# An expert's U row and V row fetched by one 8 KB gather into 16 pair buffers, with four blocks of diagonals

## Chip, cores and metric

One Trainium2 chip, of which the program uses one core. The metric is the time of the whole kernel on the device in microseconds (us); lower is better. All numbers are from timed runs or from one execution recorded by the hardware profiler.

## What is computed

A network of three layers on 256 tokens of width 1024, in float32. The part that the change touches is the expert layer at the end of the first block:

```python
# 256 tokens, 8 heads, 16 experts chosen per token and head out of 16384
ug = u_tab[ec]                     # rows of 1024 floats (4 KB)
vg = v_tab[ec]
act = gelu(einsum('thkd,td->thk', ug, xc))      # dot of each U row with its token
w = gc * act                                    # gate times activation
out = einsum('thk,thkd->td', w, vg)             # weighted sum of the V rows
```

The chosen experts come from scores against 2 x 128 sub-keys, top-16 of each half, top-16 of the 256 sums (the "routing"). What stands before it (two kinds of attention, projections) and behind it (a second block with attention, feed-forward layers) is not changed.

## The kernel before

The file is one straight program per engine, with semaphores between them. The expert stage is made of 16 **units**: unit u is one head of one half of the tokens (128 tokens, one in each partition; units 0 to 7 are tokens 0 to 127, units 8 to 15 the others). A unit has 16 experts per token, in 4 **blocks** of 4. One indirect DMA (a gather) brings, for one of the 16 experts, one row of 4 KB to each of the 128 partitions: 524,288 bytes. So a unit needs 16 gathers of U rows and 16 of V rows, 16.78 MB, and the stage 512 gathers.

Who does what for block b of unit u:

- **POOL** (GpSimd) issues the gathers, in one order: U block b of unit u, then V block b-1 (lines 644 to 667; V block 3 follows U block 0 of the next unit). U rows go to 8 buffers (`ubuf`, two blocks deep); before U block b POOL waits in `hold` until the dots of the block two before are done (`dots_done`). V rows go to 16 buffers (`vbuf`, four blocks deep); before V block b it waits until the same block of the unit before was summed (`rows_summed`, line 629). A unit's first U block also waits for its indices (`idx_ready`).
- **DVE** (VectorE) makes one dot for each gathered U row, in place in the row's buffer (line 1629, function `dot`; the tokens stand in PSUM), and between the dots, one piece behind each, the routing of the next unit and the one behind it (`route_stage`, lines 1544 to 1609; its pieces are chained by the semaphore `route_step`, raised and awaited by DVE itself). The indices of unit u+1 are done behind the fifth dot of unit u.
- **ACT** (ScalarE) turns the four dots into weights (gelu, line 928; times gate, line 933) and, in `diag` (line 942), the weights into four 128x128 diagonal matrices in `DIAG`. There are two blocks of diagonals, so `diag` of block b waits until block b-2 was summed (line 940). Once per unit it also makes the exponentials of the gates (line 924), on which DVE's `route_stage` 14 to 16 wait.
- **PE** (TensorE) adds, per gathered V row, diagonal times row into two PSUM banks (line 2333, `sum_rows`): 8 products of 128x128 by 128x512 in float32 for each block, each recorded as two instructions, and raises `rows_summed` behind the block. Before each row it waits for that row's landing (`v_loaded`).

The stage's surroundings. Unit 0 and 1 run while PE still makes queries and scores, units 2 to 15 stand in loops and, for the last two, behind them. Before unit 14 ACT and DVE do the normalization of the first half of the tokens (`norm_root`, `norm_rstd`), between units 14 and 15 they copy its transposed result (`norm_hi`, `norm_lo`). Behind unit 15 comes the input projection of the second block ("ab"): 14 pieces of weights, loaded by SP into the area that the expert rows leave, split into a high part by ACT (line 432) and a low part by DVE or POOL (line 439, 588). SP loads piece 0 when the dots of unit 15 block 2 are done, piece 1 with those of block 3 (lines 511 to 514), the others when the last V row has landed (line 515). ACT and DVE split piece 0 and 1 when block 0 and block 1 of unit 15 are summed (lines 981, 1695).

The place of things: `ROWS` is one area of 24,576 columns; `A`, `B` and the first half of `SCR` hold queries, sub-keys and scratch until the scores are made, and are free during the rest of the stage.

Of the kernel before, what the change touches and what calls it, by code (L numbers as in the profile page):

```python
# [15 lines left out]
D = 1024  # L16
# [8 lines left out]
UNITS = TT * PH  # L25
# [115 lines left out]
def build(nc, a, out, at):  # L141
    ctx = ExitStack()
    with ctx:
        sems = {}

        def sem(name):
            if name not in sems:
                sems[name] = ctx.enter_context(nc.semaphore(name))
            return sems[name]
# [119 lines left out]
        SCORE = PROJ[:, 0:4096]  # L269
        N2W = PROJ[:, 4096:5120]  # L270
        HEAD = PROJ[:, 5120:5632].rearrange("p (t n) -> p t n", t=TT)
        DIAG = PROJ[:, 5120:6144].rearrange("p (q k n) -> p q k n", q=2, k=4)
        R = PROJ[:, 6144:7168]
        r_s = R[:, 0:256].rearrange("p (q n) -> p q n", q=2)
        r_w = R[:, 256:512]
# [17 lines left out]
        ubuf = [ROWS[:, n * D:(n + 1) * D] for n in range(NU)]  # L293
        vcol = [NU + 8 * (n % 4 // 2) + 2 * (n // 4) + n % 2 for n in range(NV)]
        vbuf = [ROWS[:, c * D:(c + 1) * D] for c in vcol]
        XP_BANK = (J["peer_0"] + 6) % 8
        assert XP_BANK < 7
        XP = PS[:, XP_BANK:XP_BANK + 2, :]
# [37 lines left out]
        xn_ready = [sem(f"xn_ready{t}") for t in range(TT)]  # L336
        u_loaded = [sem(f"u_loaded{n}") for n in range(NU)]
        v_loaded = [sem(f"v_loaded{n}") for n in range(NV)]

# [114 lines left out]
        def _(sp):  # L454
# [53 lines left out]
            sp.wait_ge(*pieces["query", 1].used)  # L508
            for n in range(6, 8):
                load("query", n)  # L510
            sp.wait_ge(sem("dots_done"), 4 * UNITS - 1)
            load("ab", 0)
            sp.wait_ge(sem("dots_done"), 4 * UNITS)
            load("ab", 1)
            sp.wait_ge(v_loaded[NV - 1], 16 * UNITS)
            for p in range(2, 14):
                load("ab", p)
            sp.wait_ge(sem("h_logf"), 1)
# [61 lines left out]
        def _(pool):  # L580
# [45 lines left out]
            def values(u, q, b, first=False):  # L626

                if not first:
                    hold("rows_summed", u * 4 + (b - 3))
                elif b == 1:  # L630
                    for p in (6, 7):
                        w = pieces["query", p]
                        pool.wait_ge(hi_ready[w.h], w.count)
                        pool.wait_ge(lo_ready[w.h], w.count)
                else:
                    pool.wait_ge(*pieces["query", (0, 1, 6, 7)[b]].used)
                for k in range(4):
                    n = 4 * b + k
                    nc.gpsimd.indirect_dma_start(  # L639
                        out=vbuf[n], out_offset=None, in_=a["peer_v"][0],  # L640
                        in_offset=bass.IndirectOffsetOnAxis(ap=r_idx[:, q, n:n + 1], axis=0)
                    ).then_inc(v_loaded[n], 16)

            def unit(u, q, first=False, second=False):
# [21 lines left out]
                if first:  # L666
                    values(u, q, 3, first)

            unit(0, 0, first=True)
            unit(1, 1, second=True)  # L670
            with pool.Fori(1, UNITS // 2) as i:
                unit(i * 2, 0)
                unit(i * 2 + 1, 1)
            values(UNITS - 1, 1, 3)

            pool.wait_ge(sem("rows_summed"), 4 * UNITS)
            for p in (2, 3, 5, 7, 9, 11, 13):
# [42 lines left out]
        def _(act):  # L720
# [216 lines left out]
            def diag(u, b, wait=True):  # L937
                act.wait_ge(sem("weights_ready"), u * 4 + (b + 1))
                if wait:
                    act.wait_ge(sem("rows_summed"), u * 4 + (b - 1))  # L940
                for k in range(4):
                    ins = nc.scalar.activation(DIAG[:, b % 2, k, :], ident, ACT.Copy, scale=r_wt[:, b % 2, k:k + 1])  # L942
                ins.then_inc(sem("diag_ready"), 1)

            def act_unit(u, q, last=False):
# [21 lines left out]
            query_cols(7)  # L967
            for b in range(2, 4):
                weights(0, 0, b)
                diag(0, b)  # L970
            act_unit(1, 1)
            with act.Fori(1, UNITS // 2 - 1) as i:
                act_unit(i * 2, 0)
# [3 lines left out]
            norm_hi(2, 0)  # L977
            act_unit(UNITS - 1, 1, last=True)

            for p in halves(0):  # L980
                act.wait_ge(sem("rows_summed"), 4 * UNITS - 3 + p)
                split("ab", p)
            sqrt_table()
            act.wait_ge(sem("rows_summed"), 4 * UNITS - 1)
            split("ab", 2)
            norm_hi(2, 1)
            norm_root(2, 1, added(J["peer_1"]), added(J["peer_1"] + 1))
            act.wait_ge(sem("rows_summed"), 4 * UNITS)
            for p in range(3, 10):
                split("ab", p)  # L990

# [195 lines left out]
        def _(v):  # L1187
# [435 lines left out]

            def dot(u, b, k, tokens=XP):

                n = (4 * b + k) % NU
                rows = ubuf[n].rearrange("p (m n) -> p m n", m=2)
                v.wait_ge(u_loaded[n], u * 32 + 16 * (1 + b // 2))
# [62 lines left out]
            vec_unit(UNITS - 2, 0, start=False)  # L1691
            norm_lo(2, 0)
            vec_unit(UNITS - 1, 1, finish=False, start=False)
            for p in halves(0):
                v.wait_ge(sem("rows_summed"), 4 * UNITS - 3 + p)
                split_lo(v, "ab", p)
            for m in range(2):
                residual(J["peer_1"] + m, 1, m)
# [298 lines left out]
        def _(pe):  # L1997
# [323 lines left out]
            def sum_rows(u, t, last=False):  # L2321

                for b in range(4):
                    if last and b == 2:
                        for _ in range(4):
                            for acc in accs:
                                pe.matmul(acc[:, 0:S], zeros, C[:, 0:S], start=False, stop=False, skip_group_check=True)
                    pe.wait_ge(sem("diag_ready"), u * 4 + (b + 1))
                    for k in range(4):
                        n = 4 * b + k  # L2330
                        pe.wait_ge(v_loaded[n], u * 16 + 16)
                        for m in range(2):
                            ins = pe.matmul(PS[:, (J[f"peer_{t}"] + m) % 8, :], DIAG[:, b % 2, k, :],  # L2333
                                            vbuf[n][:, m * BANK:(m + 1) * BANK], start=False, stop=False, skip_group_check=True)
                    ins.then_inc(sem("rows_summed"), 1)

            for t in range(TT):
                accs = [bank(J[f"peer_{t}"] + m) for m in range(2)]
                for acc in accs:
                    pe.matmul(acc, zeros, C[:, 0:BANK], start=True, stop=False, skip_group_check=True)  # L2340
                with pe.Fori(t * PH // 2, (t + 1) * PH // 2 - t) as i:
# [314 lines left out]
```

## Time and profile before

| | |
|---|---|
| timed runs | 1562.36, 1563.62, 1566.21 us; median 1563.62 |
| the profiled execution | span from first to last instruction 1649.9 us; its device time is not given beside the span |
| span over the median | 86.3 us |
| TensorE clock, mean granted | 0.928 of full |
| busy in the span | PE 1384.1, DVE 1022.0, POOL 820.8, ACT 704.8 us |
| DMA | 414.99 MB, of which gathers 268.47 MB |
| expert stage | first gather issued at 178 us, last block summed at 943 us |

The profile is read from the page (totals, the span in 40 slices, the queues) to the stage (a table of busy time over chosen stretches, one for each unit), and from there to the single instructions in order of time with what ended the idle time before each. A releaser called "remote" is one that the trace has no record for.

### The profile page before, as it was taken

The page shows a single profiled execution, that of the slowest core. Times are in us where ns is not written, and L with a number is a line of the kernel's source. Part 1 is how long each engine was busy: PE and PEld are TensorE (multiplying, and loading weights), DVE is VectorE, ACT ScalarE, POOL GpSimd, SP SyncE. Part 2 cuts the span into 40 slices and gives each one's busy share as a digit, 9 for nine tenths or more (in the row PEclk, how much of TensorE's full clock was granted, in tenths as well). Part 3 has the DMA queues.
Part 4 walks back from the last instruction along what each step waited for, and adds up shares of the span by engine and source line. Part 5 has one row for each costly group of instructions (what it writes and reads, how often), then busy time and mean ns, then how long its engine had stood idle before and what let it go on. Part 6 is the DMA issues. An engine that isn't in the chain of part 4 may idle for free.

```text
span 1649.9 us, 18659 instructions
## 1 busy us (share of the span) xinstructions
PE 1384.1 (84%) x5985; PEld 974.4 (59%) x5985; DVE 1022.0 (62%) x1923; ACT 704.8 (43%) x1374; POOL 820.8 (50%) x789
## 2 busy tenths in 40 slices
PE   7999986566775876765566899999999998999998
PEld 6777942222332332332232487979888877888887
DVE  4986875665565655655544454766885478488833
ACT  5445521321222221222232337247764657576634
POOL 2332767566766666666646462105552533164514
PEclk9999998778887888887788999999999999999999
DMA  8294899999999999999979961156766552277650
GB/s 316 71 193 145 278 355 375 342 364 392 364 357 366 356 364 372 357 349 351 349 270 374 358 222 32 51 154 188 209 190 210 179 205 77 77 209 199 208 206 26
DMA packets 217026, 414.99 MB, mean 252 GB/s; under 512 B 13210, under 2 KB 117250, under 8 KB 216962
## 3 DMA queue, kind: packets, MB, share of 16 engines
q0 software_dynamic: 73728, 268.47, 42.7%
q1 hardware_dynamic: 143090, 145.66, 28.7%
q8 instruction: 37, 0.61, 0.2%
q14 instruction: 27, 0.22, 0.0%
q10 hardware_dynamic: 144, 0.04, 0.0%
HBM read 409.93 MB, written 4.19 MB: 251 GB/s over the span
## 4 chain that ended last, share of the span: by engine, by line
PE 35%; another core or an unknown queue 20%; DVE 9%; ACT 9%; issue 8%; POOL 4%; DMA 1%; POOLq 0%; ACTq 0%; DVEq 0%
PE ps L2500 9%; PE ps L2333 5%; PE ps L2049 5%; PE ps L2501 5%; PE ps L2051 5%; PE ps L2050 5%; DVE expert_rows L1629 3%; ACT proj L942 2%; POOL weights_lo L588 2%; ACT weights_hi L432 2%; ACT proj L933 1%; DVE weights_lo L439 1%; POOL ple_proj_lo L588 1%; DMA expert_rows<-in_peer_v,route_idx 1%
## 5 line engine op out<-in xcount | busy, mean ns | idle before, releaser
L2333 PE MATMUL ps<-expert_rows,proj 128*128 128x512 f32 x1024 | 487.8, 638 | 223.8 <-ACT proj L942 182.0
L2333 PEld LDWEIGHTS ps<-expert_rows,proj 128*128 128x128 f32 x1024 | 208.0, 206 | 502.9 <-issue 320.2
L1629 DVE CUSTOM_DVE_ANT_0 expert_rows<-expert_rows,ps 128x1024 f32<-128x1024 f32 x240 | 290.2, 1212 | 116.3 <-DMA expert_rows<-in_peer_u,route_idx 87.1
L588 POOL TENSOR_TENSOR weights_lo<-weights_raw,weights_hi 128x512 fp32r<-128x512 f32 x120 | 160.2, 1369 | 364.3 <-ACT weights_hi L432 322.3
L658 POOL DMA_INDIRECT expert_rows<-in_peer_u,route_idx x256 | 249.9, 976 | 130.8 <-issue 77.7
L639 POOL DMA_INDIRECT expert_rows<-in_peer_v,route_idx x256 | 247.7, 967 | 132.0 <-issue 73.4
L942 ACT ACTIVATE proj<-consts,proj 128x128 f32<-128x128 f32 x256 | 81.8, 390 | 458.7 <-remote 338.1
L432 ACT CAST weights_hi<-weights_raw 128x2048 fp32r<-128x2048 f32 x98 | 185.5, 1916 | 103.5 <-PE ps L2051 79.1
L2500 PE MATMUL ps<-x_normT,weights_hi 128*128 128x512 f32 x640 | 222.5, 392 | 0.0
L439 DVE TENSOR_TENSOR weights_lo<-weights_raw,weights_hi 128x2048 fp32r<-128x2048 f32 x68 | 161.5, 2381 | 73.2 <-ACT weights_hi L432 72.8
L2049 PE MATMUL ps<-weights_hi,x_normT 128*128 128x512 f32 (+1 forms) x496 | 188.4, 380 | 10.2 <-DVE weights_lo L439 3.9
L2051 PE MATMUL ps<-weights_hi,x_normT 128*128 128x512 f32 (+1 forms) x496 | 184.8, 373 | 0.0
L2050 PE MATMUL ps<-weights_lo,x_normT 128*128 128x512 f32 (+1 forms) x496 | 184.6, 372 | 0.0
L2501 PE MATMUL ps<-x_normT,weights_lo 128*128 128x256 f32 x640 | 179.2, 280 | 0.0
L2500 PEld LDWEIGHTS ps<-x_normT,weights_hi 128*128 128x128 f32 x640 | 119.7, 187 | 26.3
L2501 PEld LDWEIGHTS ps<-x_normT,weights_lo 128*128 128x128 f32 x640 | 121.0, 189 | 0.0
L2049 PEld LDWEIGHTS ps<-weights_hi,x_normT 128*128 128x128 f32 x496 | 93.4, 188 | 32.3 <-issue 4.4
L2051 PEld LDWEIGHTS ps<-weights_hi,x_normT 128*128 128x128 f32 x496 | 93.4, 188 | 16.7
L2050 PEld LDWEIGHTS ps<-weights_lo,x_normT 128*128 128x128 f32 x496 | 93.5, 189 | 15.5 <-issue 0.2
L1861 DVE SCALAR_TENSOR_TENSOR work_a<-ps,conv_cols,work_a 128x254 f32<-128x254 f32 (+1 forms) x176 | 76.5, 476 | 29.2 <-ACT work_a L1077 25.1
L695 POOL TENSOR_TENSOR hidden_hi<-work_a 128x256 f32 (+1 forms) x44 | 41.9, 951 | 100.2 <-ACT work_a L1057 100.0
L2049 PE MATMUL ps<-weights_hi,hidden_hi 128*128 128x512 f32 x176 | 68.7, 390 | 0.0
(340 smaller groups left out, 1959.3 us busy)
## 6 DMA issues: line engine op xcount, KB each, us to landing
weights_raw<-in_ffn_up SPq DMA_DIRECT2D x88, 512.0 KB, 5.0
weights_raw<-in_ffn_down SPq DMA_DIRECT2D x22, 1024.0 KB, 4.9
weights_raw<-in_ab_w_in SPq DMA_DIRECT2D x14, 1024.0 KB, 5.2
weights_raw<-in_w_in SPq DMA_DIRECT2D x12, 1024.0 KB, 9.2
weights_raw<-in_ple_gate SPq DMA_DIRECT2D x8, 1024.0 KB, 6.2
weights_raw<-in_c_w_in SPq DMA_DIRECT2D x6, 1024.0 KB, 6.2
weights_raw<-in_w_out SPq DMA_DIRECT2D x4, 1024.0 KB, 17.7
weights_raw<-in_peer_w_query SPq DMA_DIRECT2D x4, 1024.0 KB, 8.2
```

What stands on the lines that cost most here:

```text
L432: copy(w.hi[:, :], w.raw[:, :]).then_inc(hi_ready[w.h], 1)
L439: eng.tensor_tensor(w.lo[:, :], w.raw[:, :], w.hi[:, :].bitcast(F32), ALU.subtract).then_inc(lo_ready[w.h], 1)
L588: ins = pool.tensor_tensor(w.lo[:, c], w.raw[:, c], w.hi[:, c].bitcast(F32), ALU.subtract)
L639: nc.gpsimd.indirect_dma_start(out=vbuf[n], out_offset=None, in_=a["peer_v"][0], in_offset=bass.IndirectOffsetOnAxis(ap=r_idx[:, q, n:n + ...
L658: nc.gpsimd.indirect_dma_start(out=ubuf[n], out_offset=None, in_=a["peer_u"][0], in_offset=bass.IndirectOffsetOnAxis(ap=r_idx[:, q, 4 * b ...
L1629: ins = nc.vector.tensor_tensor_reduce(out=rows, in0=rows, in1=tokens, scale=1.0, scalar=0.0, op0=ALU.mult, op1=ALU.add, accum_out=r_dot[: ...
L2049: pe.matmul(o, x[0], w[0], start=first, stop=False)
L2050: pe.matmul(o, x[0], w[1], start=False, stop=False)
L2051: return pe.matmul(o, x[1], w[0], start=False, stop=last)
L2333: ins = pe.matmul(PS[:, (J[f"peer_{t}"] + m) % 8, :], DIAG[:, b % 2, k, :], vbuf[n][:, m * BANK:(m + 1) * BANK], start=False, stop=False, ...
L2500: pe.matmul(b.rearrange("p (a t) -> p a t", a=2), hi[:, c, g, :], x_both(c), start=c == 0, stop=False)
L2501: ins = pe.matmul(b[:, 0:S], lo[:, c, g, :], XHI[:, c, :], start=False, stop=c == KC - 1)
```

## The change

A new input, `peer_uv`, holds for each expert its U row and its V row side by side (8 KB). Units 0 and 1 work as before. From unit 2 to unit 14 one gather brings the pair for one expert, so a unit has 16 gathers, of 1,048,576 bytes each. There are 16 pair buffers of 8 KB per partition, four blocks deep: four of them in `A`, `B` and `SCR`, twelve in `ROWS`. Before block b POOL waits until the same block of the unit before was summed. Unit 15 (`last_unit`) again gathers U and V rows apart, each into its half of a pair buffer, in the order of before. `DIAG` has four blocks, so ACT's `diag` waits for the block four before. PE waits for V landings in units 0, 1 and 15 alone. The first loads of "ab" wait until block 1 of unit 15 is summed, and their splits until block 2 is, since these areas now hold pairs.

```diff
-        DIAG = PROJ[:, 5120:6144].rearrange("p (q k n) -> p q k n", q=2, k=4)
+        DIAG = [x[:, n * BANK:(n + 1) * BANK].rearrange("p (k n) -> p k n", k=4)
+                for x in (PROJ[:, 5120:6144], SCR[:, 2048:3072]) for n in range(2)]
...
+        pair_buf = [A[:, 0:HALF], A[:, HALF:2 * HALF], B[:, 0:HALF], SCR[:, 0:HALF]]
+        pair_buf += [ROWS[:, n * HALF:(n + 1) * HALF] for n in (0, 1, 2, 3, 4, 8, 5, 9, 6, 10, 7, 11)]
...
-            sp.wait_ge(sem("dots_done"), 4 * UNITS - 1)
-            load("ab", 0)
-            sp.wait_ge(sem("dots_done"), 4 * UNITS)
-            load("ab", 1)
-            sp.wait_ge(v_loaded[NV - 1], 16 * UNITS)
+            sp.wait_ge(sem("rows_summed"), 4 * UNITS - 2)
+            for p in halves(0):
+                load("ab", p)
+            sp.wait_ge(v_loaded[NV - 1], 48)
...
+            def pairs(u, q, first=False):
+
+                hold("idx_ready", u + 1)
+                for b in range(4):
+                    if first and b == 0:
+                        pool.wait_ge(pe_done, END["score_rest"])
+                    elif first and b == 1:
+                        pool.wait_ge(sem("dots_done"), 4 * u)
+                    else:
+                        hold("rows_summed", 4 * u if first and b == 3 else u * 4 + (b - 3) + (1 if first else 0))
+                    for k in range(4):
+                        n = 4 * b + k
+                        gather(pair_buf[n], a["peer_uv"], q, n, pair_loaded[n])
+
+            def last_unit(u, q):
+
+                pool.wait_ge(sem("idx_ready"), u + 1)
+                for b in range(5):
+                    if b < 4:
+                        pool.wait_ge(sem("rows_summed"), u * 4 + b - 3)
+                        for n in range(4 * b, 4 * b + 4):
+                            gather(pair_buf[n][:, 0:D], a["peer_u"][0], q, n, pair_loaded[n])
+                    if b > 0:
+                        for n in range(4 * b - 4, 4 * b):
+                            gather(pair_buf[n][:, D:2 * D], a["peer_v"][0], q, n, v_loaded[n])
+
             unit(0, 0, first=True)
             unit(1, 1, second=True)
-            with pool.Fori(1, UNITS // 2) as i:
-                unit(i * 2, 0)
-                unit(i * 2 + 1, 1)
-            values(UNITS - 1, 1, 3)
+            values(1, 1, 3)
+            pairs(2, 0, first=True)
+            pairs(3, 1)
+            with pool.Fori(2, UNITS // 2 - 1) as i:
+                pairs(i * 2, 0)
+                pairs(i * 2 + 1, 1)
+            pairs(UNITS - 2, 0)
+            last_unit(UNITS - 1, 1)
...
             def diag(u, b, wait=True):
                 act.wait_ge(sem("weights_ready"), u * 4 + (b + 1))
                 if wait:
-                    act.wait_ge(sem("rows_summed"), u * 4 + (b - 1))
+                    act.wait_ge(sem("rows_summed"), u * 4 + (b - 3))
...
+            act.wait_ge(sem("rows_summed"), 4 * UNITS - 1)
             for p in halves(0):
-                act.wait_ge(sem("rows_summed"), 4 * UNITS - 3 + p)
                 split("ab", p)
             sqrt_table()
-            act.wait_ge(sem("rows_summed"), 4 * UNITS - 1)
+            act.wait_ge(sem("rows_summed"), 4 * UNITS)
             split("ab", 2)
...
+                    rows = pair_buf[n][:, 0:D]
+                    v.wait_ge(pair_loaded[n], u * 16 - 16)
...
                     for k in range(4):
                         n = 4 * b + k
-                        pe.wait_ge(v_loaded[n], u * 16 + 16)
+                        if early or last:
+                            pe.wait_ge(v_loaded[n], 48 if last else u * 16 + 16)
+                        rows = vbuf[n] if early else pair_buf[n][:, D:2 * D]
...
+    given += [("peer_uv", _np.concatenate([inputs["peer_u"][0], inputs["peer_v"][0]], 1))]
```

## Rows read from the trace of the kernel before

**Rows 1.** The page: DMA busy in 40 slices of the span, in tenths.
```profile
DMA  8294899999999999999979961156766552277650
```

**Rows 2.** Busy time by stretch, one row each for units 0 and 5.
```profile
core 0: us, PE busy (x) PEld busy (x) DVE busy (x) ACT busy (x) POOL busy (x), PEclk, DMA share, GB/s
178.00:229.00 51.00, 43.80 (x313) 38.87 (x312) 43.67 (x87) 20.41 (x37) 41.49 (x32) 0.97 0.94 339
...
414.00:460.00 46.00, 30.50 (x65) 13.18 (x65) 26.29 (x72) 11.84 (x40) 30.83 (x33) 0.80 0.94 365
```

**Rows 3.** POOL in order of time: last gather of a run, and the next.
```profile
452.67 0.94 POOL L658 DMA_INDIRECT expert_rows<-in_peer_u,route_idx  x1 [0.30 <-issue]
459.33 0.94 POOL L639 DMA_INDIRECT expert_rows<-in_peer_v,route_idx  x1 [5.72 <-remote]
```

**Rows 4.** Busy time by stretch: DMA at full rate, and behind the hold.
```profile
437.00:457.00 20.00, 7.47 (x18) 3.04 (x16) 9.90 (x31) 0.00 (x0) 12.65 (x14) 0.75 1.03 409
457.00:462.00 5.00, 2.05 (x3) 1.02 (x4) 4.17 (x13) 3.31 (x13) 2.06 (x3) 0.50 0.44 149
```

**Rows 5.** DVE and ACT in order of time, around the hold.
```profile
443.59 0.41 DVE L1569 TENSOR_TENSOR proj<-proj 128x256 f32<-128x256 f32 x1
...
451.45 0.43 DVE L1572 MAX8 proj<-proj 128x8 f32<-128x256 f32 x1 [4.54 <-remote]
...
458.62 1.28 ACT L942 ACTIVATE proj<-consts,proj 128x128 f32<-128x128 f32 x4 [21.72 <-remote]
```

**Rows 6.** PE in order of time, and two short stretches of it.
```profile
414.01 30.45 PE L2333 MATMUL ps<-expert_rows,proj 128*128 128x512 f32 x64 [16.39 <-ACT proj L942]
...
414.00:421.00 7.00, 6.99 (x10) 3.06 (x11) 7.00 (x19) 3.13 (x14) 5.48 (x6) 0.61 0.78 263
430.00:437.00 7.00, 7.00 (x17) 3.04 (x16) 2.45 (x8) 2.22 (x9) 5.23 (x6) 1.00 1.03 414
```

**Rows 7.** POOL's waits in the stage: us in total, times, longest.
```profile
POOL expert_rows L639 <- remote: 57.7, 12, 5.7
POOL expert_rows L658 <- DVE proj L1629: 37.4, 8, 15.7
POOL expert_rows L658 <- remote: 11.3, 3, 6.2
```

**Rows 8.** The page: packet sizes; two queues (packets, MB, share of 16 engines).
```profile
DMA packets 217026, 414.99 MB, mean 252 GB/s; under 512 B 13210, under 2 KB 117250, under 8 KB 216962
...
q0 software_dynamic: 73728, 268.47, 42.7%
q1 hardware_dynamic: 143090, 145.66, 28.7%
```

**Rows 9.** One block of unit 14 on ACT and PE, in order of time.
```profile
858.02 0.20 ACT L928 ACTIVATE proj<-proj 128x4 f32<-128x4 f32 x1 [3.44 <-DVE proj L1629]
858.32 0.85 ACT L933 ACTIVATE proj<-proj 128x1 f32<-128x1 f32 x4
859.20 1.28 ACT L942 ACTIVATE proj<-consts,proj 128x128 f32<-128x128 f32 x4
...
860.53 7.13 PE L2333 MATMUL ps<-expert_rows,proj 128*128 128x512 f32 x16 [1.68 <-ACT proj L942]
```

**Rows 10.** POOL's two long holds near the end, and what DVE waited for.
```profile
858.79 0.94 POOL L658 DMA_INDIRECT expert_rows<-in_peer_u,route_idx  x1 [15.67 <-DVE proj L1629]
904.60 0.94 POOL L658 DMA_INDIRECT expert_rows<-in_peer_u,route_idx  x1 [6.29 <-DVE proj L1629]
...
851.78 0.17 DVE L1269 RECIPROCAL stats<-stats 128x1 f32<-128x1 f32 x1 [23.82 <-ACT stats L772]
```

**Rows 11.** The end of the stage: PE, ACT, DVE in order of time.
```profile
943.58 0.47 PE L2049 MATMUL ps<-weights_hi,x_normT 128*128 128x512 f32 x1
...
940.78 1.90 ACT L432 CAST weights_hi<-weights_raw 128x2048 fp32r<-128x2048 f32 x1 [5.70 <-issue]
...
942.80 2.29 DVE L439 TENSOR_TENSOR weights_lo<-weights_raw,weights_hi 128x2048 fp32r<-128x2048 f32 x1 [5.30 <-ACT weights_hi L432]
```

More of the change, by code:

```diff
@@ L338, in build @@
         v_loaded = [sem(f"v_loaded{n}") for n in range(NV)]
+        pair_loaded = [sem(f"pair_loaded{n}") for n in range(NV)]
         def cols512(m, c0, n=512):
@@ L667, in unit, with gather @@
                     values(u, q, 3, first)
+            def gather(dst, table, q, n, loaded):
+                nc.gpsimd.indirect_dma_start(
+                    out=dst, out_offset=None, in_=table, in_offset=bass.IndirectOffsetOnAxis(ap=r_idx[:, q, n:n + 1], axis=0)
+                ).then_inc(loaded, 16)
+            def pairs(u, q, first=False):
[20 more added lines that the diff above has]
+                            gather(pair_buf[n][:, D:2 * D], a["peer_v"][0], q, n, v_loaded[n])
             unit(0, 0, first=True)
             unit(1, 1, second=True)
-            with pool.Fori(1, UNITS // 2) as i:
-                unit(i * 2, 0)
-                unit(i * 2 + 1, 1)
-            values(UNITS - 1, 1, 3)
+            values(1, 1, 3)
[6 more added lines that the diff above has]
+            last_unit(UNITS - 1, 1)
             pool.wait_ge(sem("rows_summed"), 4 * UNITS)
@@ L939, in diag @@
                 if wait:
-                    act.wait_ge(sem("rows_summed"), u * 4 + (b - 1))
+                    act.wait_ge(sem("rows_summed"), u * 4 + (b - 3))
                 for k in range(4):
-                    ins = nc.scalar.activation(DIAG[:, b % 2, k, :], ident, ACT.Copy, scale=r_wt[:, b % 2, k:k + 1])
+                    ins = nc.scalar.activation(DIAG[b][:, k, :], ident, ACT.Copy, scale=r_wt[:, b % 2, k:k + 1])
                 ins.then_inc(sem("diag_ready"), 1)
@@ L969, in _ @@
                 weights(0, 0, b)
-                diag(0, b)
+                diag(0, b, wait=False)
             act_unit(1, 1)
@@ L987, in _ @@
             norm_root(2, 1, added(J["peer_1"]), added(J["peer_1"] + 1))
-            act.wait_ge(sem("rows_summed"), 4 * UNITS)
             for p in range(3, 10):
@@ L1624, in dot @@
             def dot(u, b, k, tokens=XP):
-                n = (4 * b + k) % NU
-                rows = ubuf[n].rearrange("p (m n) -> p m n", m=2)
-                v.wait_ge(u_loaded[n], u * 32 + 16 * (1 + b // 2))
+                n = 4 * b + k
+                if isinstance(u, int) and u < 2:
+                    rows = ubuf[n % NU]
+                    v.wait_ge(u_loaded[n % NU], u * 32 + 16 * (1 + b // 2))
+                else:
+                    rows = pair_buf[n][:, 0:D]
+                    v.wait_ge(pair_loaded[n], u * 16 - 16)
+                rows = rows.rearrange("p (m n) -> p m n", m=2)
                 ins = nc.vector.tensor_tensor_reduce(out=rows, in0=rows, in1=tokens, scale=1.0, scalar=0.0,
@@ L1693, in _ @@
             vec_unit(UNITS - 1, 1, finish=False, start=False)
+            v.wait_ge(sem("rows_summed"), 4 * UNITS - 1)
             for p in halves(0):
-                v.wait_ge(sem("rows_summed"), 4 * UNITS - 3 + p)
                 split_lo(v, "ab", p)
@@ L2328, in sum_rows @@
                     pe.wait_ge(sem("diag_ready"), u * 4 + (b + 1))
+                    early = isinstance(u, int) and u < 2
                     for k in range(4):
                         n = 4 * b + k
-                        pe.wait_ge(v_loaded[n], u * 16 + 16)
+                        if early or last:
+                            pe.wait_ge(v_loaded[n], 48 if last else u * 16 + 16)
+                        rows = vbuf[n] if early else pair_buf[n][:, D:2 * D]
                         for m in range(2):
-                            ins = pe.matmul(PS[:, (J[f"peer_{t}"] + m) % 8, :], DIAG[:, b % 2, k, :],
-                                            vbuf[n][:, m * BANK:(m + 1) * BANK], start=False, stop=False, skip_group_check=True)
+                            ins = pe.matmul(PS[:, (J[f"peer_{t}"] + m) % 8, :], DIAG[b][:, k, :],
+                                            rows[:, m * BANK:(m + 1) * BANK], start=False, stop=False, skip_group_check=True)
                     ins.then_inc(sem("rows_summed"), 1)
@@ L2340, in _ @@
                     pe.matmul(acc, zeros, C[:, 0:BANK], start=True, stop=False, skip_group_check=True)
-                with pe.Fori(t * PH // 2, (t + 1) * PH // 2 - t) as i:
+                for u in range(0 if t else 2):
+                    sum_rows(u, t)
+                with pe.Fori(PH // 2 if t else 1, (t + 1) * PH // 2 - t) as i:
                     sum_rows(i * 2, t)
```

## Prediction, made before the changed kernel was run

> **What bounds the kernel now.** I read the page first: DMA is busy nine tenths and more through the slices of the expert stage and idle or half idle elsewhere, where PE is full [rows 1]. So the stage (763 us of the span, first gather to last landing) is where the change can count, and it is made of transfers. Next the table by unit: a middle unit takes 46 us, in which DVE works 26, PE 30, ACT 12, POOL 31 us, and the DMA engines 94% at 365 GB/s [rows 2]. No computing engine is full. Then single instructions. POOL issues a gather every 1.245 us (0.94 plus 0.30 of idle) [rows 3]: 32 of them are 39.8 us. The DMA engines at their fullest, share 1.03, move 409 GB/s [rows 4]: 16.78 MB are 41.0 us. These two are nearly equal, and a unit is 46 because POOL then holds 5.72 us [rows 3]. It holds once in most units, 69 us in 15 holds, beside 37.4 us in 8 holds for DVE's dots [rows 7], and the DMA engines run dry behind it (share 0.44, 149 GB/s) [rows 4].
>
> What the hold waits for is strange. DVE's MAX8 at 451.45 needs only the semaphore that DVE's own instruction of 443.59, ended at 444.00, raised; it starts 7.4 us later. ACT's diagonals at 458.62 waited 21.7 us for a sum that PE's records end by 444.5 [rows 5, 6]. Both come through "remote", in the stretch where DMA is at full rate, and POOL is released just when the engines run dry. So in this execution semaphores arrive late while DMA is full. I take this for an effect of recording, because the span is 86.3 us above the median of the timed runs, and the holds called remote are 69 us, with more behind them at unit 14. A timed run then spends 763 - 86.3 = 676.7 us in the stage. It can be checked: unit 0 as recorded, 51 us (POOL's issues are longer there) [rows 2], and 15 units at 41.0 are 666; 10.7 us are left for holds that are real. **A timed unit is thus bound by the DMA engines at about 41.0 us, with POOL at 39.8 just under it**, and not by the holds that fill the profile. I therefore make the sum against the 1563.6 of the timed runs; against the profiled 1649.9 the same terms would give 86 us more at each place, if recording costs as much again. This is the step I trust least, and the first rival takes its opposite.
>
> **POOL.** Units 2 to 14, 13 units, have 16 gathers in place of 32: POOL's issue falls from 39.8 to 19.9 us per unit if a pair costs as much as a row (as many indices and rows; the size alone differs), at most 39.8 again if an 8 KB row is written as two. On a timed run's path this is nothing at either end, since DMA needs 41.0; but POOL can now run ahead, and what it waits for is no longer the dots.
>
> **DMA.** The bytes of a unit stay. The packets fall from 32 x 128 rows and 32 x 16 semaphore writes to half of both, 2304 fewer, 144 per engine. What does one cost beyond its bytes? The queue of the gathers holds 73,728 packets of 3,641 bytes in the mean and took 42.7% of 16 x 1649.9 us: 152.9 ns each. The other has 143,090 of 1,018 bytes in 28.7%: 52.9 ns each [rows 8]. The line through both is 38.1 ns per 1,000 bytes and 14 ns per packet. That is the upper bound, as small packets also wait. The lower one comes from the full rate: at 409 GB/s an engine takes 160 ns for 4,096 bytes, of which 156 are bytes by that slope, so 4 ns. I take the middle, 9 ns: 144 x 9 = 1.3 us per unit (0.6 to 2.0), 13 x 1.3 = **-17 us** (-8 to -26). Unit 41.0 becomes 39.7.
>
> Two statements of the Trainium skill, DMA: Bandwidth & Descriptors, bear on this. Its section on where 436 GB/s comes from says that for HBM to SBUF the HBM side binds at about 358 GB/s; by that a unit would be 46.9 us before and after, and packets would be worth nothing; the 409 GB/s of [rows 4] speak against it for this core alone. The same section has the ports end at 435 GB/s; by that a unit could not fall under 38.6 us, and 13 units would give at most 31 us.
>
> **Depth.** Before, U runs two blocks ahead, and the queue is shallow, since POOL is only 3% faster than DMA. DVE's pauses reach POOL and then DMA: 15.67 us before unit 14, where DVE stood 23.8 us for ACT's root, and 6.29 at unit 15 [rows 10]. After, a block's four buffers are refilled when it is summed, with three blocks, 3 x 9.9 = 29.7 us of transfers, still to come. From landing to sum it takes: last dot 1.2 and a routing piece 0.7, gelu, weights, diagonals 0.20 + 0.85 + 1.28, PE 7.1 [rows 9], 11.4 us, and POOL's 1.2 to the first refill. If PE stands at its lower clock, a block costs 7.0 / 10 x 16 = 11.2 us at a granted 0.61 and by that up to 13.7 at 0.5 [rows 6]: 19 us. At full clock 29.7 - 12.6 = 17 us are left, more than either hold as recorded; at the lower clock 10, more than the shorter. So the real part of these holds goes. Of the 10.7 us left over above, 7 us may be a hold in unit 0 to 1, which stays; I take **-5 us** for the rest (0 to -11).
>
> PE itself: 4 x 6.9 = 27.5 us per unit at full clock against 39.7 us, 70%. It was 30.5 in 46 with the clock falling each time it stood for 16 us [rows 2, 6]; with a block every 9.9 us its pauses are 3 us. It would bound only at the low clock held throughout (55 us), which its own work prevents: over a stretch that starts 16 us later it is 1.00 again [rows 6]. DVE has 26 and ACT 12 us of work per unit [rows 2]. The four blocks of diagonals cost no instruction; ACT's wait for PE moves two blocks back.
>
> **The seam at unit 2.** V block 3 of unit 1 now goes ahead of unit 2, whose first pair block waits for the scores (long made), the second for unit 1's dots, the third and fourth for its last sum. The U rows of those dots are issued 12 gathers (15 us) before POOL asks; the last sum comes 2.3 + 7.1 = 9.4 us behind the last dot [rows 9], while the first two pair blocks hold 19.8 us of transfers. I take 0 for a gap, at most 3 us. Queued behind that wait are only POOL's own gathers.
>
> **The end.** Unit 15 has the order and bytes of before. Piece 0 of "ab" is loaded later and piece 1 earlier (both at the sum of block 1), and both are split behind the sum of block 2: 1.9 + 1.9 + 2.3 = 6.1 us against 7.1 us of PE for block 3 [rows 9, 11]. Before, piece 1 was cast at 940.78 and its low part came at 942.80, while PE began at 943.58 [rows 11]. The cover is block 3; if the loads come late, piece 1 gates PE. Within -1 to +4 us; I take 0.
>
> Sum: 1563.6 - 17 - 5 = **1542 us**, ends 1563.6 - 26 - 11 = 1527 and 1563.6 - 8 + 7 = 1563.
>
> **The rivals.** *Late semaphores are real, and now never drained.* For: [rows 3 to 6]; DMA will be full without a pause, and recovery came only when it ran dry. If a timed run has them, a block's way from landing to refill is 13 + 21 = 34 us, over the 29.7 us that are covered; it decides from about 17 us of lateness on. A unit would take 9.9 + 34 + 3 = 47 us against 41: +78 us for 13 units, 1640 us. Against: the 676.7 us leave no room for them before. 8%.
>
> *A row still moves as before.* If a gather's 8 KB row is cut into two 4 KB packets, or bytes alone set the rate, the packets save nothing but semaphore writes, and only the depth is left: 1563.6 - 0 to -5, 1560 us. For: nearly all packets are under 8 KB [rows 8], so no gather shows the price. Against: 217,026 - 216,962 = 64 are 8 KB or more, so such packets exist. The Trainium skill (same page, section SWDGE vs HWDGE vs iDMA) prefers packets of at most 4096 B. By that POOL would need 39.8 us again too. 12%.
>
> *8 KB packets or the seam and end cost more than they give*, a few us slower: 1563.6 + 10, 4%. *The timed run had holds of its own*: then up to 676.7 - (51 + 41 + 13 x 39.0 + 41) = 37 us go, 1527. This is in my range and has 10%.
>
> **How the numbers follow.** The forecast has 66%. A measurement of this kernel can tell about 0.3%, 4.7 us. Faster: 66 + 10 and 3 of the second rival, 79%; same: its other 9%; slower: 8 + 4, 12%. The range 1526 to 1565 holds the forecast's bounds, the deep gain and the second rival, and leaves out the first.
>
> **What the changed profile would show.** POOL's gathers at 1.24 us, 16 per unit, and long waits for PE's sums (over 15 us per unit), not for dots. DMA share 1.0 with about 420 GB/s in any 20 us of units 3 to 14; no dip near unit 14; the first load of "ab" behind a PE sum. Recorded semaphores may still come late there, and its span may stand above its timed runs by 80 us or more. I am wrong if POOL's gather takes 1.9 us, if the rate stays at 409, if the timed gain is near 80 us (then the holds were real), or if units end in waits at a full DMA.

## The result, and the profile after

The changed kernel takes **1548.39 us** in the median (4 runs, 1547.70 to 1549.62), beside 1562.99 us (4 runs, 1561.88 to 1566.21) for the kernel before on the same chip: ratio 0.9895, interval 0.9873 to 0.9918. The forecast was 1542, its range 1526 to 1565. The profiled execution has a span of 1547.8 us and its own time is 1549.62 us, so this time nothing lies between profiled and timed runs.

The page of the changed kernel: DMA busy in 40 slices, the sizes of packets and the queue of the gathers (packets, MB, share of 16 engines), and the group of the pair gathers (count, busy us, mean ns, idle before it).

```profile
DMA  9286699999999999999999500557665443476650
...
DMA packets 187077, 415.00 MB, mean 268 GB/s; under 512 B 9883, under 2 KB 113923, under 8 KB 160387
...
q0 software_dynamic: 43776, 268.45, 42.3%
...
L674 POOL DMA_INDIRECT expert_rows<-in_peer_uv,route_idx x156 | 148.3, 951 | 229.7 <-PE ps L2379 193.4
```

Against [rows 1] the weak slice near unit 14 is gone. The slices are of different lengths (41.2 us before, 38.7 after), so they are compared by shape alone. Against [rows 8] the queue of the gathers lost 29,952 packets, which is 13 units x 2304: an 8 KB row moves as one packet. A pair gather holds POOL for 951 ns, no more than a row of 4 KB in [rows 3].

Busy time by stretch, changed kernel: the seam, a stretch of the middle, and the last stretch, where unit 15 gathers its rows apart again.

```profile
270.00:345.00 75.00, 59.46 (x124) 24.37 (x122) 47.26 (x122) 19.61 (x65) 31.05 (x34) 0.93 1.01 421
...
385.00:425.00 40.00, 29.93 (x64) 12.39 (x64) 27.38 (x70) 12.35 (x41) 15.15 (x16) 0.96 1.01 421
...
785.00:825.00 40.00, 33.74 (x77) 15.61 (x78) 25.02 (x48) 13.11 (x52) 24.34 (x26) 0.91 1.02 410
```

Each stretch of 40 us from 345 to 785 shows 420 to 422 GB/s, where [rows 4] has 409 at its fullest. Cut at every 16.78 MB of landed rows, units 2 to 14 take 39.8 to 40.0 us each. POOL's waits in the stage (us in total, times, longest) and some of its gathers in order of time:

```profile
POOL expert_rows L674 <- PE ps L2379: 196.2, 40, 8.2
POOL work_a L674 <- PE ps L2379: 69.8, 13, 9.1
```

```profile
344.07 1.10 POOL L674 DMA_INDIRECT expert_rows<-in_peer_uv,route_idx  x1 [3.54 <-PE ps L2379]
345.47 0.94 POOL L674 DMA_INDIRECT expert_rows<-in_peer_uv,route_idx  x1 [0.30 <-issue]
346.71 0.93 POOL L674 DMA_INDIRECT expert_rows<-in_peer_uv,route_idx  x1 [0.30 <-issue]
347.95 0.94 POOL L674 DMA_INDIRECT expert_rows<-in_peer_uv,route_idx  x1 [0.30 <-issue]
355.70 0.94 POOL L674 DMA_INDIRECT expert_rows<-in_peer_uv,route_idx  x1 [6.81 <-PE ps L2379]
```

POOL now waits 266 us for sums, about 20 us per unit, and it costs nothing: DMA has share 1.01 all the while. No wait is called remote in this trace from 270 to 830 us, against 69 us of such holds in [rows 7] alone.

### The profile page after: what moved, and what is told of

The parts are those of the page before. It is cut to its first block, busy times and chain, and to the rows that moved or that the text cites. A ratio compares the mean times of both kernels' runs of the same rounds, so it can differ in the third digit from the quotient of the medians.

```text
span 1547.8 us, 18260 instructions
## 1 busy us (share of the span) xinstructions
PE 1387.3 (90%) x5985; PEld 971.1 (63%) x5985; DVE 1032.8 (67%) x1923; ACT 707.7 (46%) x1374; POOL 622.3 (40%) x581
## 4 chain that ended last, share of the span: by engine, by line
PE 51%; DMA 21%; DVE 9%; POOL 7%; ACT 6%; issue 5%; ACTq 0%; POOLq 0%; DVEq 0%
DMA expert_rows<-in_peer_uv,route_idx 15%; PE ps L2548 10%; PE ps L2379 9%; PE ps L2092 7%; PE ps L2094 7%; PE ps L2093 7%; DMA scratch<-in_peer_uv,route_idx 5%; PE ps L2549 5%; DVE weights_lo L443 2%; POOL weights_lo L591 2%; POOL expert_rows L642 2%; ACT weights_hi L436 1%; POOL expert_rows L674 1%; PE ps L2057 1%; POOL expert_rows L661 1%
## 5 line engine op out<-in xcount | busy, mean ns | idle before, releaser
L1672 DVE CUSTOM_DVE_ANT_0 expert_rows<-expert_rows,ps 128x1024 f32<-128x1024 f32 x184 | 224.1, 1220 | 142.6 <-DMA expert_rows<-in_peer_uv,route_idx 131.6
L2379 PE MATMUL ps<-expert_rows,scratch 128*128 128x512 f32 x512 | 241.9, 629 | 58.3 <-ACT scratch L981 58.3
L674 POOL DMA_INDIRECT expert_rows<-in_peer_uv,route_idx x156 | 148.3, 951 | 229.7 <-PE ps L2379 193.4
L2379 PEld LDWEIGHTS ps<-expert_rows,scratch 128*128 128x128 f32 x512 | 100.6, 201 | 198.6 <-issue 118.9
L967 ACT ACTIVATE proj<-proj 128x4 f32<-128x4 f32 x64 | 13.2, 206 | 402.1 <-DVE proj L1672 402.1
L2379 PE MATMUL ps<-expert_rows,proj 128*128 128x512 f32 x288 | 136.9, 632 | 27.4 <-ACT proj L981 27.4
L2379 PEld LDWEIGHTS ps<-expert_rows,proj 128*128 128x128 f32 x288 | 57.1, 202 | 107.4 <-issue 69.2
L2379 PE MATMUL ps<-work_a,proj 128*128 128x512 f32 x112 | 62.8, 713 | 33.6 <-ACT proj L981 33.6
```

The source lines that it names most:

```text
L674: nc.gpsimd.indirect_dma_start(out=dst, out_offset=None, in_=table, in_offset=bass.IndirectOffsetOnAxis(ap=r_idx[:, q, n:n + 1], axis=0)). ...
L2379: ins = pe.matmul(PS[:, (J[f"peer_{t}"] + m) % 8, :], DIAG[b][:, k, :], rows[:, m * BANK:(m + 1) * BANK], start=False, stop=False, skip_gr ...
```

## The experiments

The runs were made on three chips, each beside runs of the kernel before on the same chip. On the first the kernel before takes 1565.33 us (17 runs, 1561.31 to 1568.46), on the second 1663.36 us (11 runs, 1651.89 to 1675.33), on the third 1655.31 us (15 runs, 1643.20 to 1663.86). That difference turned out to be the main finding. On which chip the first result was measured is not on record. Its times for the kernel before, 1561.88 to 1566.21 us, are those of the first chip, and the text counts it with that one.

### The kernel before once more, on the first chip

> The kernel before, unchanged, profiled a second time. Theory A (the late semaphores and POOL's hold of 5.7 us per unit belong to that one recording, a timed run does not have them): the timed run is again 1562 to 1566 us, and if this recording is clean its span is within 3 us of that, its middle units take 40.9 to 41.2 us, POOL's waits called remote are gone, and the last gather lands near 852 us. Theory B (the holds are part of the kernel): the span is again near 1650 us with units of 46 us, while the timed run stays at 1563, and then only recording can explain the 86 us.

Measured: 2285.11 us (1 run). In it the chip granted TensorE a mean clock of 0.556, so it says nothing of the 1563 us. No wait of its stage is called remote, but DMA is at 0.93 there and not full. It gives one price:

```profile
500.00:549.00 49.00, 49.00 (x65) 14.48 (x64) 25.77 (x69) 11.60 (x39) 30.34 (x32) 0.56 0.93 338
```

At 0.56, close to the lower of the two clock levels, PE is busy for all of the 49 us and a unit takes 49.1 us. The prediction had 55 us for a PE held at its low clock, but that was for a granted 0.5: its 27.5 us of work at full clock, divided by 0.56, are 49 us.

### Two 4 KB gathers in place of one of 8 KB, first chip

```diff
-                        gather(pair_buf[n], a["peer_uv"], q, n, pair_loaded[n])
+                        gather(pair_buf[n][:, 0:D], a["peer_u"][0], q, n, pair_loaded[n])
+                        gather(pair_buf[n][:, D:2 * D], a["peer_v"][0], q, n, pair_loaded[n])
```

> The changed kernel, but each pair fetched by two gathers of 4 KB rows, U and V, into the two halves of the same pair buffer; buffers, waits and four blocks of diagonals as in the change. Theory packets (the gain is the longer row: 39.8 instead of 41.0 us per unit): 13 units x 1.2 = 16 us come back, 1562 to 1566 us, units of 40.9 to 41.1 us. Rival depth (the gain is POOL running ahead and the deeper buffers): it keeps most of the gain, 1548 to 1553 us.

Measured: 1563.52 us (8 runs), ratio 0.9981 (0.9970 to 0.9992) to the kernel before. One stretch, and POOL's waits for PE in the stage:

```profile
340.00:380.00 40.00, 30.97 (x63) 12.62 (x62) 26.07 (x61) 12.11 (x39) 30.16 (x33) 0.91 1.03 410
```

```profile
POOL expert_rows L674 <- PE ps L2380: 8.5, 12, 3.6
POOL work_a L674 <- PE ps L2380: 6.5, 4, 3.9
```

All that the change has but the 8 KB gather is here, and the rate is 410 GB/s and a unit 41.0 us, as before. So the 1.2 us per unit come from the 8 KB rows, not from buffers or waits. Cut by landed rows, this kernel takes 801.9 - 269.0 = 532.9 us from the start of unit 2 to that of unit 15, and the changed one 787.9 - 270.2 = 517.7 us: 15.2 us in 13 units, 1.17 us each.

### Four blocks of diagonals alone, first chip

```diff
-        DIAG = PROJ[:, 5120:6144].rearrange("p (q k n) -> p q k n", q=2, k=4)
+        DIAG = [x[:, n * BANK:(n + 1) * BANK].rearrange("p (k n) -> p k n", k=4)
+                for x in (PROJ[:, 5120:6144], SCR[:, 2048:3072]) for n in range(2)]
...
-                    act.wait_ge(sem("rows_summed"), u * 4 + (b - 1))
+                    act.wait_ge(sem("rows_summed"), u * 4 + (b - 3))
```

> The kernel before with the four blocks of diagonals alone. Theory packets: no change, 1562 to 1565 us. Rival depth (ACT's early wait for PE held the stage back): 3 to 8 us faster, 1555 to 1560 us.

Measured: 1567.81 us (10 runs), ratio 1.0014 (1.0002 to 1.0027): worth nothing. This is also the first readable profile of the old order of gathers on this chip: a stretch, and POOL's waits in the stage other than its own issue.

```profile
500.00:541.00 41.00, 32.58 (x71) 13.91 (x70) 26.13 (x68) 12.01 (x39) 30.71 (x32) 0.89 1.03 409
```

```profile
POOL expert_rows L659 <- DVE proj L1630: 9.1, 8, 1.6
POOL expert_rows L640 <- DVE proj L1630: 4.0, 13, 0.3
```

Its own time is 1564.13 us. It was profiled too, and yet every unit from 1 to 14 takes 40.9 to 41.1 us, no wait is called remote, no hold for dots is longer than 1.6 us, and nothing dips before unit 14. So recording alone does not make the holds of [rows 3]. That the four diagonals took them away is the rival, and the same kernel on the third chip, below, speaks against it.

### Two blocks of diagonals in the changed kernel, first chip

```diff
-                    act.wait_ge(sem("rows_summed"), u * 4 + (b - 3))
+                    act.wait_ge(sem("rows_summed"), u * 4 + (b - 1))
...
-                    ins = nc.scalar.activation(DIAG[b][:, k, :], ident, ACT.Copy, scale=r_wt[:, b % 2, k:k + 1])
+                    ins = nc.scalar.activation(DIAG[b % 2][:, k, :], ident, ACT.Copy, scale=r_wt[:, b % 2, k:k + 1])
```

> The changed kernel with two blocks of diagonals instead of four. Theory packets: PE works 30 of 40 us in blocks of 7.1 us that come every 9.9 us, so ACT never waits for the block two before; no change, 1547 to 1550 us. Rival depth: 3 us and more are lost, over 1551 us.

Measured: 1546.98 us (4 runs), ratio 0.9877 (0.9860 to 0.9893): no worse than the change itself. ACT waits for DVE's dots in both (349.7 and 352.3 us from 300 to 820), so the diagonals of two blocks before are long free.

This run shows where the changed kernel's profiled execution loses 3 us behind the stage. PE in order of time, first the changed kernel, then this one, in the same short products of the second block:

```profile
971.11 0.49 PE L2215 MATMUL ps<-proj,expert_rows 128*128 128x128 f32 x2
971.53 0.43 PE L2219 MATMUL ps<-expert_rows,work_b 128*64 128x128 f32 x2
971.89 0.80 PE L2215 MATMUL ps<-proj,expert_rows 128*128 128x128 f32 x2
...
978.65 1.97 PE L2057 MATMUL ps<-consts,x_norm 128*128 128x128 f32 x8
```

```profile
971.34 0.49 PE L2215 MATMUL ps<-proj,expert_rows 128*128 128x128 f32 x2
...
975.27 1.09 PE L2057 MATMUL ps<-consts,x_norm 128*128 128x128 f32 x8
```

A pair of products goes from 0.49 to 0.80 us in the middle of a row of equal ones: from 971 to 980 the changed kernel was granted 0.55, this one 1.00. The first run with two gathers has the same fall at 986 us, without the 8 KB rows. Whether the other runs of the change had it is not known: they take 1547.70 to 1548.89 us, those with two blocks of diagonals 1546.80 to 1548.82.

### The kernel before on the second chip

> The kernel before, unchanged, once more, since the recording before it fell on a chip that granted 0.556 of the clock throughout. Theory A (POOL's hold of 5.7 us per unit belonged to the first recording alone): span within 3 us of the timed 1562 to 1568, middle units of 41.0 us, no wait of POOL called remote, last landing near 852 us, as the kernel with four blocks of diagonals alone already showed. Theory B: units of 46 us again.

Measured: 1667.66 us (1 run), and the 11 runs beside it, which left no profile, take 1651.89 to 1675.33 us. So here the long time is the kernel's, recorded or not. Its units 3 to 13 take 45.4 to 48.9 us. POOL's waits in the stage:

```profile
POOL expert_rows L639 <- remote: 54.1, 14, 5.5
POOL expert_rows L658 <- DVE proj L1629: 51.8, 14, 15.7
POOL expert_rows L658 <- remote: 18.2, 6, 5.3
```

They are like those of [rows 7]. Waits called remote are real on this chip and absent on the first; that a late semaphore stands behind one is shown closely further down.

### The changed kernel on the second chip

> The changed kernel, unchanged, for comparison on the same chip. 1547 to 1550 us, units of 39.8 us. If TensorE's low clock after unit 14 and in the second block was chance, it need not be in this recording, and the span is then up to 5 us shorter.

Measured: 1557.38 us (6 runs, 1551.41 to 1561.72), ratio 0.9369 (0.9329 to 0.9409): **a gain of 6.3% where the first chip gave 1.0%.** POOL's waits in its stage:

```profile
POOL expert_rows L674 <- PE ps L2379: 193.1, 37, 12.1
POOL work_a L674 <- PE ps L2379: 70.6, 12, 8.4
```

Waits called remote end in this trace around the seam, from 269 to 284 us (ACT once 17.51 us, POOL once 2.35 us); the last 4 KB row of unit 1 starts to move at 274. From 284 to 790 us, where only pairs move, there is one more, of 0.2 us at DVE. Units 1 and 2 take 45.4 and 41.9 us against 40.9 and 40.0 on the first chip, the others 39.8 to 39.9 us as there. The clock did not fall in the short products either: from 970 to 985 us PE was granted 1.00.

Unit 15 gathers 4 KB rows again, at the full rate:

```profile
815.00:825.00 10.00, 10.00 (x24) 4.37 (x23) 4.62 (x9) 2.33 (x9) 6.30 (x7) 1.00 1.03 409
```

No wait in it is called remote, and it takes 46.2 us here and 47.1 on the first chip. Two other traces of the changed kernel's variants on the slower chips have short holds of POOL there (2.4 to 3.2 us). So 4 KB rows at the full rate do not by themselves cost time on this chip. What else is needed is not shown.

### Without the zero products of unit 15, second chip

```diff
-                    if last and b == 2:
-                        for _ in range(4):
-                            for acc in accs:
-                                pe.matmul(acc[:, 0:S], zeros, C[:, 0:S], start=False, stop=False, skip_group_check=True)
```

These products add nothing; they stand in the kernel before too. In the changed kernel's trace on the first chip they lie on PE's path, since PE is behind the landings there:

```profile
815.40 7.03 PE L2379 MATMUL ps<-expert_rows,proj 128*128 128x512 f32 x16
822.27 3.62 PE L2370 MATMUL ps<-consts 128*128 128x256 f32 x16
825.72 13.90 PE L2379 MATMUL ps<-expert_rows,scratch 128*128 128x512 f32 x32
```

> The changed kernel without the eight products with zeros (3.6 us) that PE makes between block 1 and block 2 of unit 15. Theory (in the changed kernel the V rows of block 2 have landed by then, so these products lie on PE's path to the last sum): the last sum comes 2 to 3 us sooner behind the last landing, 1545.5 to 1547.5 us. Rival (the last landing sets the end in any case, as with two blocks of diagonals, or the clock falls for want of them): no change or up to 3 us slower.

Measured: 1556.97 us (6 runs), ratio 0.9369 (0.9329 to 0.9409), the same as the change. Without them PE stands idle for 3.14 us before its sums at 828.13, where the products had been, so on this chip they fill a wait. Whether they cost anything in the profile of the first chip, where PE was granted 0.68 just before, no run shows.

### Less depth, second chip

```diff
-                        hold("rows_summed", 4 * u if first and b == 3 else u * 4 + (b - 3) + (1 if first else 0))
+                        hold("rows_summed", u * 4 + (b - 1))
```

> The changed kernel, but in units 2 to 14 POOL waits before each block for the sum of the block two before, so that two blocks instead of four are in flight. Theory (a block's way from landing to refill is 11.4 + 1.2 us, which the other blocks' transfers have to cover): one block of 9.95 us covers too little, DMA runs dry, a block takes (9.95 + 12.6 + 1) / 2 = 11.8 us, a unit 47 us, the kernel 1548 + 13 x 7.3 = 1643 us, DMA share near 0.85. Rival (the refill is quicker than the records say, or PE's clock is low and makes it slower): under 1600 us, or over 1700 us.

Measured: 1744.62 us (1 run), 54.4 to 56.6 us in each of units 3 to 13. One turn of two blocks:

```profile
560.44 0.94 POOL L674 DMA_INDIRECT expert_rows<-in_peer_uv,route_idx  x1 [3.51 <-PE ps L2379]
...
577.40 0.21 ACT L967 ACTIVATE proj<-proj 128x4 f32<-128x4 f32 x1 [7.37 <-DVE proj L1672]
578.60 1.28 ACT L981 ACTIVATE proj<-consts,proj 128x128 f32<-128x128 f32 x4
...
579.93 7.13 PE L2379 MATMUL ps<-expert_rows,proj 128*128 128x512 f32 x16 [1.11 <-ACT proj L981]
...
587.99 0.94 POOL L674 DMA_INDIRECT expert_rows<-in_peer_uv,route_idx  x1 [3.71 <-PE ps L2379]
```

From a block's first gather to the gather that waits for its sum it takes 27.55 us, of which 10.6 us lie behind its last dot. The other 17.0 us are its issue, its transfer and the rest of the block before it, since POOL issues two blocks close together. Two blocks per 27.5 us are 55 us per unit, not the 47 expected from 12.6 us per way. The time is the one that the rival gave (over 1700 us), but its reason, a low clock, is not in these rows, since sums of 7.13 us are PE's at full clock. The same kernel with b - 2 in place of b - 1, on the third chip:

> The change, but POOL waits before block b for the sum of the block three before in place of the block four before, so only two blocks of transfers (2 x 9.95 = 19.9 us) cover the way from a block's last landing to its refill. By my 12.6 us for that way there is no hold that empties the queues and the time is that of the change, 1547 to 1560 us. With two blocks (the run before this) a block took 13.7 us in place of 9.95, so the way was about 27 us with one block still to come, or what was late there was something else. By 27 us, two covered blocks leave 7 us per block open and a unit takes (19.9 + 27 + about 0) / 3 x ... about 9.95 x 4 x 27 / 19.9 = 54 us at the worst, 1650 us or more; in between, 1560 to 1600 us, the way is 14 to 20 us.

Measured: 1550.07 us (1 run), units of 39.8 to 40.0 us from unit 3 on. One block more of depth takes back all of it. So by this run three blocks would do, and the fourth of the change is reserve.

### What keeps the change fast on the slower chips

Three kernels again, on the third chip, beside 1655.31 us for the kernel before. Two gathers in place of one:

> The change with its U and V row fetched by two gathers of 4 KB, a second time. On a chip where the kernel before takes 1561 to 1568 us it should again take about 1564. The run is for a chip where the kernel before takes 1650 us or more: there the changed kernel took 1557, and three things of it could protect it. If it is the new buffers and waits (POOL waits only for PE's sums, three blocks deep), this kernel has them too and takes 1565 to 1580 us. If it is the halved number of gathers, packets and semaphore writes, this kernel does not have that, POOL has again 39.8 us of gathers in a 41.0 us unit, and it takes 1630 to 1670 us. My guess is 60 to 40 for the buffers and waits.

Measured: 1640.08 us (7 runs), ratio 0.9921 (0.9878 to 0.9964). The guess, 60 to 40 for buffers and waits, was wrong. Four diagonals in the kernel before:

> The kernel before with four blocks of diagonals, a second time. On a chip where the kernel before takes 1561 to 1568 us: no change. Where it takes 1650 us or more: if the late diagonals alone (ACT waiting for PE) make POOL's holds, it falls to below 1600 us; if the holds come from dots and sums told late to POOL, as I think, it stays within 1 % of the kernel before.

Measured: 1640.78 us (9 runs), ratio 0.9925 (0.9889 to 0.9961), within the 1% expected. Two diagonals in the changed kernel:

> The change with two blocks of diagonals, a second time. On either kind of chip within 0.5 % of the change itself, 1545 to 1565 us, if the four blocks are worth nothing; above 1580 us on a chip where the kernel before takes 1650 us, if the two further blocks are what makes the change robust.

Measured: 1556.77 us (4 runs), ratio 0.9410 (0.9352 to 0.9468), as the change. The kernel with two gathers has the four diagonals too, so its 0.8% are no more than theirs: the new buffers and the new order add nothing here that can be told from noise. The rest of the 6% comes with the 8 KB gather, which the last of the three kernels has and the first two have not. The second also answers the rival left open on the first chip: with four diagonals, holds called remote are there all the same (POOL 50.8 us in 10 holds). The trace of the run with two gathers on this chip shows a hold closely: POOL, PE, DVE and ACT, each in order of time, and then two stretches by busy time.

```profile
549.46 0.94 POOL L674 DMA_INDIRECT expert_rows<-in_peer_v,route_idx  x1 [0.31 <-issue]
555.97 0.94 POOL L674 DMA_INDIRECT work_a<-in_peer_u,route_idx  x1 [5.57 <-remote]
...
529.21 5.15 PE L2380 MATMUL ps<-work_a,proj 128*128 128x512 f32 x8 [5.18 <-ACT proj L982]
534.20 1.88 PE L2380 MATMUL ps<-work_b,proj 128*128 128x512 f32 x4
535.91 1.88 PE L2380 MATMUL ps<-scratch,proj 128*128 128x512 f32 x4
...
546.99 0.08 DVE L1673 DVE_READ_ACCUMULATOR2_ANT proj<- 128x1 f32 x1
...
553.69 0.21 ACT L968 ACTIVATE proj<-proj 128x4 f32<-128x4 f32 x1 [14.35 <-remote]
```

```profile
530.00:550.00 20.00, 14.93 (x32) 6.03 (x30) 10.97 (x29) 2.33 (x9) 15.12 (x17) 0.93 1.03 410
550.00:556.00 6.00, 0.00 (x0) 0.00 (x0) 3.09 (x9) 2.17 (x9) 0.43 (x2) 0.50 0.86 342
```

The block in `work_a`, `work_b` and `scratch` was summed by 537.8. POOL was ready to refill it at 550.4 and went on at 555.97, 18.2 us behind the sum. Its other condition, the indices of the next unit, was met at 529.3. ACT's gelu came 6.6 us behind its last dot. DMA is at 1.03 up to 550, and both go on only when it is at 0.86. The changed kernel with two diagonals, on the same chip and at the same place of a unit:

```profile
576.16 1.88 PE L2379 MATMUL ps<-scratch,proj 128*128 128x512 f32 x4
...
578.87 0.94 POOL L674 DMA_INDIRECT work_a<-in_peer_uv,route_idx  x1 [3.72 <-PE ps L2379]
```

There the refill comes 0.8 us behind the sum, with DMA at 1.01 and 422 GB/s. What stays open is which part of the 8 KB gather does it. It halves the row packets, the semaphore writes of the queues and POOL's issuing at once; no run here separates them. Nor does a run show what makes a semaphore late, or in what the chips differ.

## Why the prediction was right, and where it was wrong

**The time and the bound: right.** A unit is bound by the DMA engines at 41.0 us with POOL just under it; the run with four diagonals shows 41.0 us and DMA at 1.03. That the timed comparison fell on a chip of the first kind is luck. On the second chip the changed kernel's 1557 us are still in the range, but the gain of 21 us that was forecast is 106 us there.

**The cause given for the 86.3 us: wrong.** The step that failed is "I take this for an effect of recording, because the span is 86.3 us above the median of the timed runs". Two chips on which this kernel takes 1643 to 1675 us in every run stand in its place, on one of them with the same holds in its trace. That the kernel of [rows 2 to 7] was recorded on such a chip is the plain reading, though its own time was not given. The difference between a profile and the timed runs was evidence that two conditions existed, not that one of them was the profiler's. The rival "late semaphores are real" had the right cause; it had the wrong outcome (1640 us), since in the stretch of 8 KB rows hardly a wait is late though DMA is full. The sign "I am wrong if the timed gain is near 80 us" did come, as 106 us, on the second chip.

**Packets: right, 15.2 us for 17.** 1.17 us per unit over 144 packets per engine is 8.1 ns each; the middle of 4 and 14 ns had been 9. One packet of 8 KB takes 313 ns in the median and one of 4 KB, in the run with two gathers, 161 ns, and the rate goes from 410 to 421 GB/s. The rival "a row still moves as before" falls with the packet count. The Trainium skill, DMA: Bandwidth & Descriptors, section SWDGE vs HWDGE vs iDMA, prefers packets of at most 4096 B; here 8 KB ones are the faster by 2.9% and need half of POOL's issues. The 358 GB/s that the Trainium skill gives for HBM to SBUF (same page, section Where 436 GB/s comes from) did not bind, as 421 GB/s show; its 435 for the ports was not reached.

**Depth: smaller than taken, and not where it was taken.** 2.9 us for 5: the last row lands at 852.0 us with the old order and at 849.1 with two gathers into the new buffers, one trace each. In timed runs these buffers are worth 1.8 us against the kernel before (1565.33 to 1563.52). Of the 2.9 us, 2.4 lie in unit 15 (49.6 us from its start to the last landing against 47.2), and none at the holds of [rows 10], which this chip doesn't have. The 5 us had no firm ground: 10.7 us less the 7 that may stay would have been 3.7.

**The seam: right.** POOL holds 6.84 us at 281.89, and DMA stays at 1.01 from 270 to 345.

**The end: 0 taken, 0 found in the stage.** From the last landing to the last sum it takes 4.6 us before (four diagonals) and 4.5 after. PE was granted 0.68 from 805 to 815 us, and its sums then run behind the landings. Behind it the low clock at 971 to 980 takes about 3 us. The sum on one profile each, from four diagonals in the kernel before to the change: last landing 852.0 to 835.0, -17.0; clock +3; -14. The times of these two executions are 1564.13 and 1549.62 us, -14.5. Of the 6 us between the forecast and the result, 2 are packets and 2 depth. The low clock would make up the rest, but it is read from one execution, and that the median run had it is not shown.

**PE and the way to a refill.** PE at a granted 0.56 takes 49.1 us per unit, which is the prediction's sum at that clock; its 55 us were for 0.5, which no run held. The way of 12.6 us from landing to refill was right for the part behind the dots, but counted from the gather it is 27.5 us when POOL issues in pairs of blocks; the three blocks of cover hide it with 29.7, and even two did.

## What to carry to other kernels

When rows that are used together lie apart in memory, put them side by side and gather them by one transfer: per byte it costs fewer packets, and it halves the issuing of a POOL that stood at 97% of the DMA time. When a profile and the timed runs differ by some per cent, time the kernel on another chip before the difference is put down to recording. And judge a change of a kernel with full DMA queues on more than one chip, as the same edit gave 1.0% on one and 6.3% on another.

## What the runs showed of the hardware that was not expected

- One program, three chips: 1561 to 1568 us on one and 1643 to 1675 us on the two others. On these, semaphores between engines arrive late while the DMA engines move 4 KB gathers at share 1.03: on the third chip POOL went on 18.2 us behind the sum that it waited for. In the stretch of 8 KB gathers, at 1.01, it was 0.8 us. One unit of 4 KB gathers at 1.03, unit 15 of the changed kernel, showed no such wait on the second chip.
- A gather of 128 rows holds POOL for 0.94 us and 0.30 of idle whether the rows have 4 or 8 KB.
- One run had TensorE at 0.556 of its clock from beginning to end and took 2285 us, while the kernel's 17 other runs on that chip stood at 0.95 to 0.98.
